# Two convolution layers of a fused network: the variance taken about the first chunk's mean, with sums formed chunk by chunk

## The reference, cut to what matters

```python
def layernorm(x, g, b):
    mu = jnp.mean(xf, axis=-1, keepdims=True)
    var = jnp.mean(jnp.square(xf - mu), axis=-1, keepdims=True)
    y = (xf - mu) * lax.rsqrt(var + EPS)
    return y.astype(x.dtype) * g + b

def conv_module(h, w_in, b_in, dw_w, dw_b, ln_g, ln_b, w_out):
    a, gt = jnp.split(h @ w_in + b_in, 2, axis=-1)
    u = a * jax.nn.sigmoid(gt)
    u = dwconv(u, dw_w, dw_b)          # 31 taps along the tokens, each channel by itself
    u = layernorm(u, ln_g, ln_b)
    return jax.nn.silu(u) @ w_out
```

## Time and profile before

| | |
|---|---|
| median of three runs | 3207.31 us (3207.24 to 3208.67) |
| the profiled execution's own time | 3207.96 us |
| its span from first to last instruction | 3206.2 us |
| mean granted clock of PE | 0.994 of full |
| busy: PE, DVE, ACT, POOL | 3140.6, 1434.8, 1253.0, 1541.4 us |

### The profile page before, as it was taken

The page is one execution under the profiler, slowest core; times in us unless marked ns, Lnnn a source line. Parts: engine busy times, 40 slices in busy tenths (PEclk is TensorE's granted clock), DMA queues, the critical chain, the costliest instruction groups (busy, mean ns, idle before and its releaser), DMA issues. The chain is left out here.

```text
span 3206.2 us, 34864 instructions
## 1 busy us (share of the span) xinstructions
PE 3140.6 (98%) x13869; PEld 2464.9 (77%) x13869; DVE 1434.8 (45%) x2666; ACT 1253.0 (39%) x1854; POOL 1541.4 (48%) x764
## 2 busy tenths in 40 slices
PE   8999999999999999999999999999999999899999
PEld 5668888865788887778888877787888886588887
DVE  5564111289543345446243523322534359753433
ACT  5463222255443335554343322222434344643332
POOL 3225554567354553334554533343455447555544
PEclk9999999999999999999999999999999999899999
DMA  5212323221232233222323322222332331133232
GB/s 183 76 47 88 103 92 99 92 71 55 73 104 89 96 105 102 89 86 92 99 92 99 111 72 66 73 86 72 93 99 92 99 95 63 40 92 105 92 99 86
DMA packets 80674, 286.03 MB, mean 89 GB/s; under 512 B 9088, under 2 KB 9344, under 8 KB 80384
## 3 DMA queue, kind: packets, MB, share of 16 engines
q1 hardware_dynamic: 80512, 283.80, 27.7%
HBM read 281.40 MB, written 2.10 MB: 88 GB/s over the span
## 5 line engine op out<-in xcount | busy, mean ns | idle before, releaser
L2267 POOL TENSOR_TENSOR WL<-RAW,WH 128x1024 fp32r<-128x1024 f32 x504 | 1216.2, 2415 | 1266.3 <-ACT WH L1581 1266.1
L1344 PE MATMUL PS<-XH,WH 128*128 128x512 f32 x2640 | 1070.6, 406 | 24.4 <-POOL WL L2267 22.1
L1345 PE MATMUL PS<-XL,WH 128*128 128x512 f32 x2640 | 1030.3, 390 | 0.0
L1346 PE MATMUL PS<-XH,WL 128*128 128x512 f32 x2640 | 1030.1, 390 | 0.0
L1581 ACT ACTIVATE WH<-RAW 128x1024 fp32r<-128x1024 f32 x504 | 529.3, 1051 | 545.9 <-PE PS L1346 457.0
L1344 PEld LDWEIGHTS PS<-XH,WH 128*128 128x128 f32 x2640 | 496.9, 188 | 169.8 <-issue 41.8
L1345 PEld LDWEIGHTS PS<-XL,WH 128*128 128x128 f32 x2640 | 497.1, 188 | 112.6 <-issue 16.1
L1346 PEld LDWEIGHTS PS<-XH,WL 128*128 128x128 f32 x2640 | 496.7, 188 | 105.6
L1344 PE MATMUL PS<-HH,WH 128*128 128x512 f32 x1264 | 495.3, 392 | 9.6 <-DVE HL L2165 9.6
L1345 PE MATMUL PS<-HL,WH 128*128 128x512 f32 x1264 | 493.4, 390 | 0.0
L1346 PE MATMUL PS<-HH,WL 128*128 128x512 f32 x1264 | 493.2, 390 | 0.0
(11 more groups left out here) (229 smaller groups left out, 2375.9 us busy)
## 6 DMA issues: line engine op xcount, KB each, us to landing
RAW<-wst SPq DMA_DIRECT2D x504, 512.0 KB, 3.5
BI<-natb SPq DMA_DIRECT2D x16, 384.0 KB, 4.6
X<-xin SPq DMA_DIRECT2D x16, 256.0 KB, 5.1
X<-cmpw SPq DMA_DIRECT2D x1, 2048.0 KB, 9.8
out<-X SPq DMA_DIRECT2D x8, 256.0 KB, 2.0
BI<-relm SPq DMA_DIRECT2D x4, 448.0 KB, 10.0
PRM<-prm SPq DMA_DIRECT2D x1, 685.0 KB, 12.4
BI<-rope SPq DMA_DIRECT2D x2, 256.0 KB, 3.9
```

Of the source, the lines that this page charges most:

```text
L1344: e.matmul(o, wh, h, start=first, stop=False)
L1345: e.matmul(o, wh, l, start=False, stop=False)
L1346: t = e.matmul(o, wl, h, start=False, stop=last)
L2267: e.tensor_tensor(WL[:, b % NSPLIT, :], RAW[:, b % NRAW, :], WH[:, b % NSPLIT, :].bitcast(f32), SUB).then_inc(*did(lo_made, ("lo", b)))
```

## The change

- `pool_tap`: the convolution's bias is added in the first of ACT's tap products and no longer in DVE's first tap.
- After chunk 0, `pivot`: PE multiplies it by ones, ACT copies the bank divided by 128 into a tile p. Chunks 0 and 1 have p subtracted on DVE (`less_pivot`); for later chunks DVE's first tap subtracts it.
- Squares (ACT) are issued 13 tiles and sums (PE, of values except chunk 0's, and of squares) 18 tiles after each chunk's finish, so all but the last chunks' lie inside the layer. The variance is the mean of squares less the square of the mean (`mean_square` on ACT, `ln_rsqrt` on DVE and ACT).
- `join_last`: for the last chunk the order becomes `two`, `own`, PE's bank, POOL's sum.
- `keep_warm`: two products of constants are issued on PE before the last chunk's finish and four after its sums.
- The centring is issued chunk by chunk between the scalings of the output loop.

```diff
+            def keep_warm(n):
+                bank = banks.get()
+                i = step("warm", bank.ap, bank.free, n)
+                bank.done((i, "mm"))
+
...
                         i = step("pool_tap", s.ap, (ch["u"], *s.free, *ch["po"].free), ch["pad"].ap[:, j0 + n:j0 + n + T],
-                                 tap(ch["c"], j0 + n), ch["po"].ap, None if n == 0 else before, ch.get("po_made"))
+                                 tap(ch["c"], j0 + n), pcol("conv_dw_b", 8 * ci + ch["c"]) if n == 0 else None,
+                                 ch["po"].ap, None if n == 0 else before, ch.get("po_made"))
...
                     step("dve_taps", ci, c, a, b, ch["own"].ap, ch["own"].free, ch["two"].ap, ch["two"].free, ch["pe"],
-                         ch["pad"].ap[:, j0:542], [tap(c, j) for j in range(j0, 31)], pcol("conv_dw_b", 8 * ci + c), ch["u"])
+                         ch["pad"].ap[:, j0:542], [tap(c, j) for j in range(j0, 31)], cur["p"].ap if c > 1 else None, cur["p_made"] if c > 1 else None,
+                         ch["u"])
...
-                    i = step("join", o.ap, o.free, ch["two"].ap, ch["own"].ap, ch["po"].ap, ch["po_made"], ends)
-                    ch["po"].done((i, "half"))
-                    ch["two"].done((i, "half"))
-                    ch["own"].done((i, "o"))
-                    if c == 7:
-                        i = step("join_pe", o.ap, ch["acc"].ap, (i, "o"), ch["pe"])
-                        ch["acc"].done((i, "o"))
+                    if c < 7:
+                        i = step("join", o.ap, o.free, ch["two"].ap, ch["own"].ap, ch["po"].ap, ch["po_made"], ends)
+                    else:
+                        i = step("join_last", o.ap, o.free, ch["two"].ap, ch["own"].ap, ch["acc"].ap, ch["po"].ap,
+                                 ch["po_made"], ch["pe"], ends)
+                        ch["acc"].done((i, "acc"))
+                    ch["po"].done((i, "po"))
+                    ch["two"].done((i, "two"))
+                    ch["own"].done((i, "own"))
                     outs.append((o, (i, "o")))
-
-                    def mean(k=len(outs) - 1):
-                        if k == 0:
-                            cur["d"] = banks.get()
-                        cur["mean"] = (step("add_up", k, cur["d"].ap, cur["d"].free, outs[k][0].ap, outs[k][1]), "mm")
-                    if c < 7:
-                        later(mean, 16)
-                    else:
-                        mean()
+                    if c == 0:
+                        later(pivot, 13, first=True)
+                        return
+                    if c == 1:
+                        for k in range(2):
+                            o, made = outs[k]
+                            outs[k] = (o, (step("less_pivot", o.ap, cur["p"].ap, made, cur["p_made"]), "o"))
+                            later(lambda k=k: square(k), 13, first=True)
+                            later(lambda k=k: add_up(k), 18)
+                        cur["d"], cur["var"] = banks.get(), banks.get()
+                    elif c < 7:
+                        later(lambda: square(c), 13, first=True)
+                        later(lambda: add_up(c), 18)
+
+                def pivot():
+                    bank = banks.get()
+                    cur["p"] = tiles.get()
+                    i = step("pivot", cur["p"].ap, cur["p"].free, outs[0][0].ap, outs[0][1], bank.ap, bank.free)
+                    bank.done((i, "p"))
+                    cur["p_made"] = (i, "p")
+
+                def square(k):
+                    s = tiles.get()
+                    o, made = outs[k]
+                    cur["sq", k] = (s, (step("square", s.ap, o.ap, (made, *s.free)), "sq"))
+
+                def add_up(k):
+                    o, made = outs[k]
+                    if k:
+                        i = step("add_up", k == 1, k == 7, cur["d"].ap, cur["d"].free, o.ap, made)
+                        cur["mean"] = (i, "mm")
+                    s, made = cur["sq", k]
+                    i = step("add_up", k == 0, k == 7, cur["var"].ap, cur["var"].free, s.ap, made)
+                    s.done((i, "mm"))
+                    cur["squares"] = (i, "mm")
...
                 norm_end(norm)
                 pool_taps(cur["ch"], TAPS_POOL[7] // 2, TAPS_POOL[7])
                 flush()
+                step("tables")
+                keep_warm(2)
                 finish(cur["ch"])
-                step("tables")
-                var = banks.get()
-                for k, (o, made) in enumerate(outs):
-                    i = step("center", o.ap, cur["d"].ap, (made, cur["mean"]))
-                    s = tiles.get()
-                    j = step("square", s.ap, o.ap, ((i, "o"), *s.free))
-                    j = step("add_up", k, var.ap, var.free, s.ap, (j, "sq"))
-                    s.done((j, "mm"))
-                cur["d"].done((i, "o"))
-                pt_free[0] = pt_free[1] = ((j, "mm"),)
-                rs = step("ln_rsqrt", var.ap, (j, "mm"))
+                square(7)
+                add_up(7)
+                d, var, t = cur["d"], cur["var"], tiles.get()
+                keep_warm(4)
+                cur["p"].done(("tap", ci, 7, 0))
+                pt_free[0] = pt_free[1] = (cur["squares"],)
+                rs = step("mean_square", d.ap, cur["mean"], t.ap, t.free)
+                t.done((rs, "v"))
                 ys = Ring([])
                 for _ in range(2):
                     y = banks.get()
                     ys.spare.append((y.ap, y.free))
+
+                def center(k):
+                    o, made = outs[k]
+                    outs[k] = (o, (step("center", o.ap, d.ap, (made, (rs, "t"))), "o"))
+
+                def scale(k):
+                    return step("ln_scale", outs[k][0].ap, var.ap, (outs[k][1], (rs, "rs")))
+                step("ln_rsqrt", var.ap, t.ap, rs, cur["squares"])
+                for k in range(3):
+                    center(k)
                 mv = []
-                scales = [step("ln_scale", outs[0][0].ap, var.ap, (rs, "rs"))]
+                scales = [scale(0)]
                 for k, (o, _) in enumerate(outs):
                     if k < 7:
-                        scales.append(step("ln_scale", outs[k + 1][0].ap, var.ap, (rs, "rs")))
+                        scales.append(scale(k + 1))
+                    if k < 5:
+                        center(k + 3)
                     y = ys.get()
...
+                d.done(outs[7][1])
...
-            def add_up(i, k, d, d_free, o, o_made):
-                if k == 0:
+            def add_up(i, first, last, d, d_free, o, o_made):
+                if first:
                     for event in d_free:
                         w.wait_ge(*at(event))
                 w.wait_ge(*at(o_made))
-                e.matmul(d, ones, o, start=k == 0, stop=k == 7).then_inc(*did(pe_made, (i, "mm")))
+                e.matmul(d, ones, o, start=first, stop=last).then_inc(*did(pe_made, (i, "mm")))
+
+            def pivot(i, p, p_free, o, o_made, bank, bank_free):
+                for event in bank_free:
+                    w.wait_ge(*at(event))
+                w.wait_ge(*at(o_made))
+                e.matmul(bank, ones, o, start=True, stop=True).then_inc(*did(pe_made, (i, "mm")))
+
+            def warm(i, bank, free, n):
+                for event in free:
+                    w.wait_ge(*at(event))
+                w.wait_ge(*at("cst2"))
+                for _ in range(n):
+                    t = e.matmul(bank, ones, mask[:, 0:T], start=True, stop=True)
+                t.then_inc(*did(pe_made, (i, "mm")))
...
+            def pivot(i, p, p_free, o, o_made, bank, bank_free):
+                for event in p_free:
+                    w.wait_ge(*at(event))
+                w.wait_ge(*at((i, "mm")))
+                e.activation(p, bank, ACT.Copy, scale=1.0 / 128).then_inc(*did(act_made, (i, "p")))
+
+            def mean_square(i, d, mean, t, t_free):
                 ln_exp()
-                w.wait_ge(*at(made))
-                e.activation(var, var, ACT.Ln, scale=1.0 / D, bias=eps).then_inc(*did(act_made, (i, "ln")))
+                for event in t_free:
+                    w.wait_ge(*at(event))
+                w.wait_ge(*at(mean))
+                e.activation(t, d, ACT.Square, scale=1.0 / D).then_inc(*did(act_made, (i, "t")))
+
+            def ln_rsqrt(i, var, t, rs, squares):
+                w.wait_ge(*at((rs, "v")))
+                e.activation(var, var, ACT.Ln, bias=eps).then_inc(*did(act_made, (i, "ln")))
                 w.wait_ge(*at((i, "ln")))
-                e.activation(var, var, ACT.Exp, scale=-0.5).then_inc(*did(act_made, (i, "rs")))
+                e.activation(var, var, ACT.Exp, scale=-0.5).then_inc(*did(act_made, (rs, "rs")))
...
-                        e.tensor_scalar(own, pad[:, 0:T], taps[0], bias, MUL, ADD).then_inc(
-                            *did(dve_made, ("tap", ci, c, 0)))
+                        if p is None:
```

(35 more changed lines are left out.)

24 lines of the change are left out of this document (14 added, 10 removed).

## The result

The changed kernel takes 3226.72 us (median of 4 runs, 3223.85 to 3229.4) where the kernel before takes 3207.68 beside it (3207.24 to 3208.67): a ratio of 1.0059 [1.0041, 1.0076], 19 us slower. The forecast was 3213.0, its range ended at 3222. In the profiled execution (its own time 3229.4) the span is 3227.6 us against 3206.2, 21.4 more.

What follows compares the result with a forecast made beforehand. PE is busy 3140.6 of 3206.2 us, so its standing or slow running counts; DVE limits inside the layer. Layer 1 +2.7, layer 2 +1.4 and half of a possible 3.4 for the clock give +5.7: 3213.0 us, range 3198 to 3222.

Steps and rivals of the forecast that it cites:

- The pivot's bank and the 7 us of idle: Pass 6 (of 16 product blocks) waits for ACT's pivot copy; PE idles about 7 us; pass 7's product +3.6 us.
- On DVE two subtractions of the pivot are added, 1.25: Inside the layer, beside passes 6 and 7: DVE's two pivot subtractions take 1.25 us, from two operations in 1.29.
- DVE's first tap stays one operation: Inside the layer: leaving out the first chunk's sum and moving the bias to ACT change nothing on this path.
- The clock in pass 8: Inside the layer, where PE waits for the first two squares: no low clock was charged.
- The recurrence for the squares: Inside the layer, PE waits up to 2.3 us for late squares; waits add up, last scaled input +10.2 us.
- the forecast's 120.6: Forecast length in us of the stretch from a layer's first taps to its last taps, 110.4 and 110.5 before.
- The end of the layer: Last taps to next stage's first real product: 26.45 us; that product at 812.5 instead of 810.89.
- The third weight block: Next stage's start: ACT splits this block late, PE needs it at 823.4 and stands until 826.6; +2.7 us.
- (a): Rival: stalls inside the layer don't come, last scaled input +3.4, 3197.8 us; 18%.
- (b): Rival: only the pivot stalls, squares are in time, last scaled input +7, 3205 us; 15%.
- (d): Rival: table loads for squares, 2 x 1.28 us before each add, about +20, 3227 us; 4%.
- (c): Rival: short waits for squares add up to low-clock stretches, about 1.8 us each, about +12, 3219 us; 14%.

Runs made afterwards that it cites:

- a_bank: Changed kernel, but the pivot's product uses the bank that later holds the sums of squares, so pass 6 doesn't wait for its copy: 3228.39 us.
- a_nosub: Changed kernel without DVE's pivot subtractions (variance about zero); pivot's product and copy stay, the first chunk's values are summed again: 3218.7 us.
- a_nowarm2: Changed kernel without the two constant products ahead of the last chunk's finish; the four after its sums stay: 3217.52 us.
- a_late: Changed kernel, but the sums on PE are due 26 instead of 18 tiles after each chunk's finish: 3209.68 us.
- bank_late_nosub: Changed kernel with the pivot's product in the later bank of squares, sums due at 26 tiles, and no pivot subtraction on DVE: 3201.56 us.
- b_port: Kernel before, but in six chunks of each layer DVE's first tap subtracts an SBUF residual tile in place of the bias: 3217.35 us.

## Why the prediction was wrong

The direction and most single readings were right; the size inside the layer wasn't. By the forecast's own steps:

**The pivot's bank and the 7 us of idle: right in the trace, and the size at pass 7 by luck.** The wait is 6.9 us, it ends with ACT's copy, and PE restarts at the low clock. The forecast's +3.6 us at pass 7 (697.1 + 15.7 against 709.27) was nearly met, +4.1, but for another reason. DVE's two subtractions (3.16 us) and its slower first tap (1.78 instead of 0.81) make 4.1 us, and a_bank, where the idle is gone, is late by as much. In a_nosub, where the slow operations are gone, the idle shows instead: +2.8 us in layer 1 and +4.0 in layer 2, where the low clock behind it lasts longer (0.50 still from 2692 to 2694).

**"On DVE two subtractions of the pivot are added, 1.25" and "DVE's first tap stays one operation": wrong in size.** The step took the duration from an operation with a bank as one input, run with POOL at rest. With two SBUF tiles and POOL at work the two take 3.16 us, and each first tap 1.2 to 1.8 instead of 0.81. Rows that warn of it stood in the trace of before. This is DVE and POOL right behind the first convolution layer, where line 1857, with 0.49 us elsewhere, took 1.91 and line 1859, with 0.75 elsewhere, took 2.77 while POOL split weights:

```profile
843.14 1.91 DVE L1857 TENSOR_SCALAR XH<-X,PRM 128x512 fp32r<-128x512 f32 x1
845.09 2.77 DVE L1859 SCALAR_TENSOR_TENSOR XL<-X,PRM,XH 128x512 fp32r<-128x512 f32 x1
...
842.29 5.01 POOL L2267 TENSOR_TENSOR WL<-RAW,WH 128x1024 fp32r<-128x1024 f32 x2 [9.13 <-ACT WH L1581]
```

Line 1859 reads two SBUF tiles and ends at 847.86, 0.56 us after POOL's second operation (847.30). Line 1857 reads only one and is slow as well, so a second tile isn't the only thing to look for.

The Trainium skill states the rule (SBUF — State Buffer, "Who interferes with whom" and "SBUF: two separate sides"): VectorE with two SBUF inputs and a GpSimd operation that reads SBUF want the same pair of ports, and the one that comes second waits for the whole instruction of the other. The trace agrees: the two-tile operations end 0.55 or 0.56 us after the POOL operation that was running, and the POOL operation that begins beside one of them ends 1.12 to 1.15 us after it, nearly its own 1.28. So such an operation of DVE is priced by what is left of POOL's, plus 0.55 us.

**The clock in pass 8: put at nothing.** The forecast has PE wait there, but charges a low clock only behind the pivot's wait and at the layer's end. In the profiled execution PE came back from the 3.0 us wait at 0.50 in layer 1 and at 0.72 in layer 2, which cost 3.0 and 1.7 us against a_nowarm2, where the same wait left the clock up.

**The recurrence for the squares: right about PE's wait, and it left out DVE's.** It let DVE run its taps from gated input to scaled input without a pause, the 14.7 us of before. But the bank `two` holds PE's taps, and DVE adds to it. The pivot's wait, or a sum of squares that PE waits for, stands ahead of these taps. The starts of the gated inputs (DVE's timeline, layer 1), as us over the kernel before, each counted from the gated input of chunk 2:

| chunk | 3 | 4 | 5 | 6 | 7 |
|---|---|---|---|---|---|
| forecast | +3.6 | +5.4 | +5.9 | +7.7 | +10.2 |
| after | +4.1 | +11.3 | +12.3 | +14.5 | +17.6 |
| a_nowarm2 | +4.2 | +8.3 | +9.4 | +11.5 | +14.7 |
| a_nosub | +2.8 | +6.3 | +7.4 | +8.7 | +11.9 |
| a_late | +4.1 | +5.5 | +5.6 | +6.4 | +8.6 |

Nearly all of layer 1's miss, 5.4 of 7.4 us, arises in one pair, between chunks 3 and 4. The slow subtractions and the slow first tap make the scaled input late (713.85), so the sigmoid and with it the first squares (718.58) are late. PE waits 3.02 us, where the forecast's numbers leave 0.9 (730.95 less 712.85, 16.35 and 0.85), and comes back at 0.50, which is the 3.0 us more. DVE's 5.03 us for the taps at 727.00 are a consequence: in this pair they cost nothing, since DVE then waits another 1.49 us for PE's product (738.13). They make the next square late.

By size, over both layers the first stretch is 13.6 us longer than forecast, and three differences between profiled executions divide it. The clock: 3.0 and 1.7 us (after less a_nowarm2). The two-tile operations, with what follows from them at the full clock: 2.8 and 1.5 (a_nowarm2 less a_nosub). What a_nosub has over the forecast's 120.6, 1.7 and 3.0: late squares, DVE's waits for taps, and its own extra product. (The 1.25 us for the subtractions aren't to be taken off the 120.6. The forecast has them on DVE beside PE's late pass 7, and its last scaled input follows from 712.85 by way of 747.75 without them.) The parts depend on the order in which causes are taken away: a_late, with the slow operations still there, gives back 9.0 and 7.8 us, more than the whole miss. So a slow operation on DVE costs much where PE's sums wait for what it delays.

**The end of the layer: right.** 26.47 us against 26.45, with the four sums in 3.4, the two constant products in 1.7 (shown by a_nowarm2), the square and sums as listed. POOL's last tap sum ends at 808.69 (taken at 799; the last taps are 8.6 us late themselves), but the join still ends at 811.05, before PE reaches the last sums (813.60): it is covered as the forecast said, with less to spare. As an edit by itself, in the kernel before, where nothing covers it, the reordered join is worth 9.4 us (b_join).

**The third weight block: right, and the clock half by luck.** The block starts 14.05 to 14.07 us after the first real product (forecast 14.1), and the wait is 2.88 us where the clock was kept, 1.35 where it wasn't. The clock, taken at half of 3.4 us for both layers, came to nothing in layer 1 and 3.0 us in layer 2.

**The rivals.** (a) and (b) are ruled out by the waits at 698.20 and 719.25. (d) is ruled out: no table load stands beside a square inside the layer. (c), the clock, took part, with 4.7 of the 13.6 us: one low stretch a layer behind a square's wait (0.50 from 719 to 725, 0.72 from 2713 to 2719), where a_nowarm2 is granted 1.00. It followed from the late squares. What the forecast says would happen without its stalls was tried as well: without waits for squares its last scaled input is +7, a_late has +8.6; without the pivot's stall too +3.4, bank_late_nosub has +4.6, and 3201.6 us where (a) says 3197.8.

**What stays open.** How the 4.6 us of a_nosub's rest divide wasn't measured apart. Why the same wait of 3.0 us left the clock up in one execution and down in another isn't shown. A pivot with its subtraction on another engine wasn't tried.

## What to carry to other kernels

Where DVE is the limit and POOL works beside it, price an operation by a row with the same kinds of inputs at a time when POOL is busy: another SBUF tile as an input can double an operation whose count stays the same, since begun beside a POOL operation it ended 0.55 us after that one. When a wait is added in PE's in-order queue, follow everything behind the waiting product to the engines that want it; a long wait that another engine's work covers may be free (6.9 us here), while a short one (3.0 us) ahead of what the limiting engine needs costs its full length, and as much again if the clock falls behind it. A cost that shows in one profiled execution and not in the next, as the clock did here, is to be looked for in more than one trace before the rest of a miss is divided. The cheapest mend was a due time, 26 tiles instead of 18, and one part of the change, tried alone, was better than all of it.

## What the runs showed that was not expected

- The same idle time before the first real product left the clock up in one layer and down in the other: 2.19 us before 821.11 (first matmul 0.80 us) and before 2814.65 (0.50 us). The 3.0 us wait for the first squares did the same between executions: the clock fell behind it in both layers of the changed kernel and in neither of a_nowarm2.
- In b_join layer 2's squares ran at full speed behind a gap in PE of 1.55 us in place of 3.08 (7.13 us for sixteen half-products, 8.83 in layer 1), and an edit that moves a gap by 1.6 us shortened the end of the layers by 2.5 and 5.5 us.
- Two-tile operations of DVE and POOL's additions slow each other: 0.69 to 1.78 us on DVE, 1.28 to 1.55 on POOL. All 28 such operations of the changed kernel and of b_port end 0.55 or 0.56 us after the POOL operation that was running.
